# Sixteen more expert panels in the routing stage, none in a late part of the parked stage

## The reference, cut to what matters

```
q  = x @ w_q                         # 8 heads, 2 halves of 128
s1, i1 = top_k(q1 . keys1, 16)       # per token and head
s2, i2 = top_k(q2 . keys2, 16)
top_s, pos = top_k(all 256 sums s1 + s2, 16)
idx  = i1 * 128 + i2                 # one of 16384 experts
gate = softmax(top_s)
act  = gelu(expert_u[idx] . x)
out  = sum(gate * act * expert_v[idx])
```

## Time and profile before

| what | value |
|---|---|
| median of 3 runs | 3925.56 us (3922.45 to 3928.78) |
| the profiled execution | 3915.23 us, span 3913.5 us |
| mean granted clock of TensorE | 0.959 |
| PE busy | 3632.4 us, 93% of the span |
| DVE, ACT, POOL busy | 2147.4, 1508.4, 1925.0 us |

### The profile page before, as it was taken

One profiled execution on the slowest core, in us unless ns is written; L12 is line 12 of the kernel. 1 busy time (PEld: TensorE's weight loads), 2 busy tenths in 40 slices (PEclk: granted clock), 3 DMA queues, 4 the chain that ended last, 5 costly groups with the idle time before them and its releaser, 6 DMA issues. The chain is left out here.

```text
span 3913.5 us, 50588 instructions
## 1 busy us (share of the span) xinstructions
PE 3632.4 (93%) x17190; PEld 3064.6 (78%) x17190; DVE 2147.4 (55%) x3421; ACT 1508.4 (39%) x2624; POOL 1925.0 (49%) x1479
## 2 busy tenths in 40 slices
PE   7979998988999999999988989999979997689999
PEld 6457998978999999988867747888758885367887
DVE  7782997866999776643334554332243321754320
ACT  3433555743333343444323344442334321443431
POOL 4623675436788777655533414454435543014544
PEclk9989999999999999999999989999989998699999
DMA  3022453668999899433331202323213335012232
GB/s 128 22 65 76 153 172 127 226 263 321 384 405 403 329 347 345 171 99 96 93 119 61 83 11 81 97 91 93 90 62 96 95 96 127 1 33 89 93 93 90
DMA packets 172661, 569.80 MB, mean 146 GB/s; under 512 B 15458, under 2 KB 58594, under 8 KB 155013
## 3 DMA queue, kind: packets, MB, share of 16 engines
q1 hardware_dynamic: 152244, 427.68, 32.6%
q0 software_dynamic: 20304, 140.78, 9.6%
HBM read 518.33 MB, written 50.07 MB: 145 GB/s over the span
## 5 line engine op out<-in xcount | busy, mean ns | idle before, releaser
L277 POOL TENSOR_TENSOR weight_low<-weight_ring,weight_high 128x512 fp32r<-128x512 f32 x1264 | 1726.7, 1388 | 1825.7 <-ACT weight_high L249 1386.8
L291 PE MATMUL banks<-normed_high,weight_high 128*128 128x512 f32 (+1 forms) x2528 | 954.1, 377 | 61.3 <-ACT weight_high L249 32.4
L292 PE MATMUL banks<-normed_low,weight_high 128*128 128x512 f32 (+1 forms) x2528 | 943.4, 373 | 0.0
L249 ACT ACTIVATE weight_high<-weight_ring 128x512 fp32r<-128x512 f32 x632 | 398.7, 631 | 1386.6 <-PE banks L298 1301.0
L291 PEld LDWEIGHTS banks<-normed_high,weight_high 128*128 128x128 f32 x2528 | 486.4, 192 | 136.1 <-issue 48.6
L298 PE MATMUL banks<-normed_high,weight_low 128*128 128x512 f32 (+1 forms) x2528 | 573.2, 368 | 5.8 <-POOL weight_low L277 5.6
L292 PEld LDWEIGHTS banks<-normed_low,weight_high 128*128 128x128 f32 x2528 | 486.1, 192 | 62.2 <-issue 2.3
L298 PEld LDWEIGHTS banks<-normed_high,weight_low 128*128 128x128 f32 x2528 | 462.3, 188 | 67.9 <-POOL weight_low L277 9.2
L251 ACT ACTIVATE weight_high<-weight_ring 128x512 fp32r<-128x512 f32 (+1 forms) x632 | 389.8, 617 | 91.9 <-PE banks L298 81.9
L2037 DVE TENSOR_TENSOR square<-square,banks 128x512 f32<-128x512 f32 x88 | 60.5, 688 | 416.5 <-PE banks L298 414.9
L291 PE MATMUL banks<-parked_high,weight_high 128*128 128x384 f32 x768 | 262.4, 342 | 15.8 <-ACT weight_high L249 10.3
(11 more groups left out here) (371 smaller groups left out, 5650.1 us busy)
## 6 DMA issues: line engine op xcount, KB each, us to landing
weight_ring<-in_experts SPq DMA_DIRECT2D x256, 512.0 KB, 5.5
weight_ring<-in_ffn_gate SPq DMA_DIRECT2D x88, 512.0 KB, 3.5
weight_ring<-in_ffn_up SPq DMA_DIRECT2D x88, 512.0 KB, 3.5
weight_ring<-in_ffn_down SPq DMA_DIRECT2D x64, 512.0 KB, 3.5
expert_gates<-spread_space SPq DMA_DIRECT2D x6, 4096.0 KB, 12.2
parked_space<-expert_gates SPq DMA_DIRECT2D x24, 768.0 KB, 8.8
parked_space<-parked_activations SPq DMA_DIRECT2D x24, 768.0 KB, 10.6
weight_ring<-in_a_w_in SPq DMA_DIRECT2D x28, 512.0 KB, 3.5
```

What stands on the lines that cost most here:

```text
L249: m.nc.scalar.activation(m.w_hi[:, s % PARTS, 0:HALF], m.ring[:, s, 0:HALF], ACT.Copy).then_inc(m.half_high, 1)
L277: m.nc.gpsimd.tensor_tensor(m.w_lo[:, s % PARTS, at], m.ring[:, s, at], m.w_hi[:, s % PARTS, at].bitcast(FP), ALU.subtract).then_inc(done, 1)
L291: m.nc.tensor.matmul(out, w_hi, hi(c), start=(first and c == 0), stop=False)
L292: m.nc.tensor.matmul(out, w_hi, lo(c), start=False, stop=False)
```

## The change

The number of u panels that are parked stays 96, and so do their order in DRAM and the sum of all panels. Sixteen of them are computed in `route` in place of the head of `parked_experts`; the loops over LATE_PANELS there run zero times, and the row schedule shrinks by sixteen steps.

```diff
-ROUTE_PANELS = 56
+ROUTE_PANELS = 72
 SPREAD_PANELS = 24
-LATE_PANELS = 16
+LATE_PANELS = 0
 PARKED = (ROUTE_PANELS + SPREAD_PANELS + LATE_PANELS) // EXPERT_GROUP
...
                 ins.then_inc(picked.turned, 1)
-                panel_products(m, pe, U, DENSE_TOKENS)
+                if U:
+                    panel_products(m, pe, U, DENSE_TOKENS)
```

## The result

| | before | after |
|---|---|---|
| median | 3924.01 us (4 runs, 3909.23 to 3928.78) | 3979.68 us (4 runs, 3973.89 to 3989.73) |
| ratio, 95% interval | | 1.0161 [1.0136, 1.0186] |
| profiled execution, span | 3915.23, 3913.5 us | 3973.89, 3972.1 us |
| granted clock | 0.959 | 0.954 |

The change makes the kernel 55.7 us slower. The forecast was slower too, but by 22 us, and the measured time lies 10 us above the range.

What follows compares the result with a forecast made beforehand. Prediction: PE, busy 93%, bounds the kernel, with DVE and DMA also full in the parked stage. Start and moved panels -6, lag at group starts +22, experts +6 give +22 us: 3925.6 to 3947.6 us, range 3914 to 3970.

Steps and rivals of the forecast that it cites:

- Route, and the start of the parked stage: Sixteen panels add 66.6 us to route and remove 74.5 late; the uncovered parked start costs +22.6 and +1.5 for the clock.
- The hole of before goes: Head of the parked groups: group 1's gates fetched earlier, so twelve panels take 50.7 us instead of 72.7, -22.0 us.
- DVE still fits, with 0.31 us a step to spare (before 0.54): Parked steps from the second group on: DVE's work sums to 344 us in 372, on paper within PE's pace.
- A lag of about 2 us that PE pays at each of eleven group starts, +22: Parked groups: late rows put DVE behind, and PE waits for the last chunk at group starts; +22 us, chance 0.40.
- DVE sets the pace throughout: Rival for the parked groups: 88 steps at DVE's 4.65 us instead of 4.225, +37 us there, total 3967 us; chance 0.15.
- Rows that come late: Parked groups: 22 rows fetched in their dot's step, DVE waiting some 20 times for 1 to 2 us.
- Experts stage: Experts stage: 50 dots for 45, all without lead, and three steps with two dots; +6 us, bounds 0 and 15.
- DMA as the bound: Rival for the parked steps: 402 GB/s is all there is, 88 steps take 6.5% longer, +24 us, total 3950; chance 0.17.

Runs made afterwards that it cites:

- first rows later: Changed kernel with the first four gathered rows fetched in steps 1 to 4, not all in step 0: 3973.51 us, 1.0126 of before.
- the early fetch by itself: Kernel before, with the first half of group 1's gates fetched behind the eighth late panel, all else unchanged: 3910.12 us, 0.9980 of before.
- five buffers: Changed kernel with five buffers for gathered rows instead of four, so parked rows are fetched a step or more ahead: 3949.89 us, 1.0096 of before.
- where DVE's stretch is taken away: Changed kernel whose three DVE chunk instructions take their second operand from PSUM, so none reads two SBUF operands: 3940.42 us, 1.0080 of before.
- no lead at the old density: Changed kernel with the row schedule of before, fifteen rows left out, each row from the fifth fetched in its dot's step: 3969.92 us, 1.0135.
- half of the change: Kernel before with ROUTE_PANELS 64 and LATE_PANELS 8, rows at 128 in 146 steps: 3933.23 us, 1.0055 of before.
- half rows: Changed kernel fetching only the u half of each gathered row, which the add uses in place of v: 3934.41 us, 1.0059 of before.
- with 0 or 2 such rows: Changed kernel with a fifth row buffer (3949.89 us), or with PARKED_SHARE 0.7 in place of 0.8 (3983.13 us); groups 2 to 11 +36.9 and +36.3 us.
- weight a step later: Changed kernel with ACT's gelu and weight of a row moved one step on, to the add's step: 4070.05 us, 1.0402 of before.

## Why the prediction was half right

- **Route, and the start of the parked stage: right.** 65.3 us for sixteen panels (forecast 66.6). The last two gelus of route, kernel after, stand 4.16 us apart (679.82 and 683.98), as in the earlier trace rows.

Panel 0 ends 33.0 us behind the start, forecast 29.7 and 1.5 for the clock. The second half's data land later than I took, at 24.0 us behind the start and not 22.1, no sooner than the 23.4 of before, though no panel of the late part is loaded beside them. The run with the first rows later gives the reason: with them out of the way the first group is 7 us shorter. Kernel after, DVE in order of time:

```profile
941.61 0.56 DVE L1592 TENSOR_TENSOR parked_space<-parked_space 128x384 f32<-128x384 f32 x1 [5.68 <-DMA parked_space<-parked_activations]
```

- **The hole of before goes: right in sum, not for the reason given.** Group 1 takes 34.3 us (42.5 before), and no line of the waits behind it names the gates. But the early fetch by itself gave back 10 of the 22 us; the rest went with the late part, where DVE stood for rows.
- **DVE still fits, with 0.31 us a step to spare (before 0.54): this step failed.** I built a step's cost from one clean step of the earlier trace rows, with line 1592 at 0.55 us, and got 3.69 us for the kernel before. In the steps with chunk work it was 4.15, so only 0.08 were to spare, and the denser rows take 0.27. Even the row for the stage, 336.0 / 84 = 4.00, hides this, as it takes in a last group without chunks. That doesn't make the new density impossible, since part of the 4.15 is time held up by POOL: five buffers held it over single groups. It means that nothing is left to catch up with.
- **A lag of about 2 us that PE pays at each of eleven group starts, +22: the place was right, and the term was mis-sized.** It measured 53.6 us over ten starts, 5.4 each. PE did wait for line 1598 there, 32.3 us, but DVE's lag grew to as much as 10.5 us and not 2, and part of it was carried on from group to group. The lower clock behind the long waits, 17 us, stood nowhere in this term, though I had priced it for the stage's start. The rival *DVE sets the pace throughout*, to which I gave 0.15, is nearest: its pace of 4.65 us a step was measured as 4.89.
- **Rows that come late: right as the start of it, wrong as its shape.** I expected some twenty waits of DVE for rows, 1 to 2 us each; it was 8, 12.4 us in all. Once DVE is 5 to 9 us behind, the rows are there (the dots of steps 12 to 15 start 14 to 16 us behind their rows' fetch). Few waits in a trace don't mean that lateness is harmless; here they mean that it has been turned into lag.
- **Experts stage: right in sign, off by a factor of two.** +11.9 for +6, within its bounds. DVE waits for rows there 52.8 us in 36 waits, against the earlier trace rows.
- **DMA as the bound: no.** 361 GB/s, and no wait of ACT for a panel in the eighty steps; five buffers moved 416 GB/s over 67.4 us with PE never idle. It comes near only where DVE's stretch is taken away.

Of exclusion, the Trainium skill, SBUF — State Buffer, section Who interferes with whom, says that a cast can take the shared ports too and that the one who issued first keeps them to its end. The traces agree on the cast, with 3.06 us at 1002.82 beside 0.36 when alone. They don't show the order: this cast started while POOL issued a row, 0.3 us before the first split, and ended behind the second. I had used that rule for the two lines with two operands only.

What stays open: how firm the division into 17 us of missing lead and 37 of density is, since the two don't simply add (no lead at the old density alone costs 51) and each rests on one trace; and why a lag heals within a group in some kernels (half of the change, half rows) and not in others. A version with all its work in place that clearly beats the kernel before wasn't found.

## What to carry to other kernels

Take the load of an engine that is nearly full from the busy time of the steps that carry all of its work, neither from one clean step nor from the whole stage: the clean step leaves out contention that is already there, and the stage takes in steps that are lighter. Here the slack was 0.54 us a step by the clean step, 0.22 by the whole stage and 0.08 by the full steps. In a ring of in-order queues (DVE's dot, ACT's weight and rounding, POOL's split and fetch, DVE's chunk) a short wait isn't paid once: it can move everything into a phase in which two engines exclude each other in most steps, and then the loop runs at the pace of the slowest until something sparse lets it out. Before work is squeezed into fewer steps, count the transfers that lose their last step of lead (from 1 to 22 here): taking all lead away at the old density cost as much as the whole change. Giving it back doesn't undo the squeeze, though: with 0 or 2 such rows, 36 us stayed.

## What the runs showed of the hardware

- A DVE instruction that meets POOL's splits may wait through several of them: 1.5 us for one (line 1598), 3.06 for the issue of a row and two splits (line 1596), 5.16 for four (line 1592, weight a step later), where each takes 0.36 to 0.56 alone. POOL's pair grew only from 2.56 to 2.9.
- After the wait of 4.03 us PE ran at the lower clock (0.50) for a while: the eight low products took 2.75 us against 1.57 in the next panel. Eleven waits cost 32 us of idle time, and the lower clock behind the seven longest, 2.8 to 4.6 us, some 17 us of slower work.
- HBM, rows and panels together gave 405 GB/s over 335 us without the exclusion. The Trainium skill, DMA: Bandwidth & Descriptors, section Where 436 GB/s comes from, has about 358 for HBM to SBUF, as one core's half of what two share; the traces of one core at work go above it, and nearer to that section's 435.
